# First mixer with every second chunk's keys in reversed token order: one level product for two chunks

## The chip, the cores and the metric

The kernel runs on one core of a Trainium2 chip. The metric is the device time of one execution in microseconds (us). Before the change the median of three runs is 1917.88 us (1913.43 to 1923.1).

TensorE appears as PE (matrix products) and PEld (its weight loads), VectorE as DVE, ScalarE as ACT, SyncE as SP (it issues the weight transfers).

## What is computed

A two-layer decoder trunk (width 1024) takes 512 prompt tokens and 8 sequences of 4 sample tokens. Layer 0 mixes tokens by HGRN2, layer 1 by gated DeltaNet (GDN); a squared-ReLU MLP follows each. The change lies in the HGRN2 mixer, which has 8 heads with 128 key features and 128 value features:

```
S_t = diag(f_t) S_{t-1} + k_t v_t^T        o_t = S_t^T q_t        k_t = (1 - lb) sigmoid(-fz_t)

within a chunk, b = running sum of log f:
A[t, s] = sum_k q[t, k] k[s, k] exp(b[t, k] - b[s, k])     for s <= t
o       = (q exp(b)) S  +  A v
S       = exp(b_last) S +  (k exp(b_last - b))^T v
```

The decay depends on the feature k, so A is no plain product of two matrices.

## The kernel before

Features lie on the 128 partitions, the 544 tokens (T: 512 of the prompt, TP, and 32 of the samples, TS) on the free axis. The prompt is cut into NC = 4 chunks of 128 tokens.

**Levels.** A is built in seven levels, m = 1, 2, 4, ..., 64 (`LEVELS`). At level m each chunk falls into blocks of 2m tokens. The second half of a block (queries) sees its first half (keys), and both decays are taken relative to the last token of the first half, so both exponents stay at or below zero. For a level, VectorE writes the differences (`apart_levels`, lines 1487 and 1488), ScalarE takes their exponential (line 978), VectorE scales queries into `QL` (line 1493) and keys into `KL` (line 1494, `scaled`), PE multiplies (line 509, `level` in `hgrn_rec`), and VectorE copies the wanted pieces into `A` under a mask (`keep`, line 1514, `copy_predicated`). `QL` holds only the second halves, 64 columns a chunk. `KL` keeps the keys at their token's place and zeros at the second halves, so a chunk's product has 128 key rows, half of them zero, and 64 query columns: four products a level, one a chunk. All are in float32, and the hardware runs each such product as two instructions, so a level shows as x8. Levels 1 and 2 have a small product more for the samples (line 512). In the text lv1 ... lv64 are the products of a level on PE, kl1 ... kl64 the pair `QL`, `KL` on VectorE, pred1 ... pred64 the masked copies.

**The diagonal** is a product of keys and queries of each chunk (line 520) times the identity (lines 1524 and 1525).

**One turn of the head loop.** PE runs a head's levels and between them the projections of the next head (`more(n)`: n tiles of six products of 272 columns, line 411; 32 tiles a head). The order on each engine is the order of the program, and semaphores order the engines. The pieces that the text names, by turn:

- the projection of the next head is evacuated in four units: three by line 1440 into `pr` during the turn, the fourth, the values, by line 1440 into `val` at the end of the turn (`hgrn_prepare`, slot 9).
- VectorE writes the low half of each weight tile (`low`, line 1336); PE's tiles of that unit wait for it.
- the forget gate of the next head: ScalarE's chain at lines 927 to 931 (which stands behind the copies at lines 986 and 987, and these behind a small PE transpose, line 449), then VectorE at line 1431 (`fls`), 1452, and the next `low`.
- the end of a turn: the sample state update (line 1553, `snew`), the third evacuation (line 1440), pred64, the scan (1466), `Q` (1468), the next head's level-1 differences, their exponential on ScalarE (961), then the copy of the output (999), its square (1001), PE's sum over features (432, `ss`), ScalarE's reciprocal root (1007, 1011), and VectorE's `out_tail` (1387, 1390, 1392), gate and `val`.
- line 955 on ScalarE writes the next head's keys `K`; lines 1401 and 1402 write `bd`, the distance to the chunk's end.

The first head is prepared ahead of the loop, and the last head stands behind it: there PE's filler is the output projection (14 tiles), and the last levels have none.

## Time and profile before

| quantity | value |
|---|---|
| median of 3 runs | 1917.88 us (1913.43 to 1923.1) |
| profiled execution | 1921.42 us |
| its span, first to last instruction | 1919.6 us, mean granted clock 0.94 |
| PE busy / PEld busy | 1795.0 us (94%) / 1699.2 us (89%) |
| DVE busy | 1089.1 us (57%), 1960 instructions |
| ACT busy | 689.8 us (36%), 1150 instructions |
| diagonal product of the first HGRN2 head to that of the last | 52.76 to 362.45 us |
| the last head's normalised output | 405 us |

The HGRN2 heads take the stretch from about 50 us to about 405 us; the MLPs (PE alone, projections back to back) and the GDN mixer fill the rest. The granted clock is the share of 2.4 GHz that PE was given in a stretch: 1.00 is 2.4 GHz, 0.50 is 1.2 GHz. Whole-span shares say little on a stage of a fifth of the span, so the rows below come from that stage.

### The profile page before, as it was taken

How to read it: one execution, taken by the hardware profiler on the slowest of the kernel's cores; microseconds unless marked ns; L12 is line 12 of the kernel's file. 1: busy time of each engine (PE TensorE's matmuls, PEld its weight loads, DVE VectorE, ACT ScalarE, POOL GpSimd, SP SyncE). 2: the span in 40 equal slices, each digit the busy share in tenths (PEclk: the TensorE clock that was granted, in tenths of full speed). 3: DMA queues.
4: the chain of work that ended last, by engine and by line, in shares of the span. 5: the costliest groups of instructions: out<-in, count | busy, mean ns of one | idle time of the engine just before them, and what ended most of it. 6: DMA issues, size and time to landing. Idle time of an engine off the chain costs nothing. (4 is left out here: it accounts for less than half of the span.)

```text
span 1919.6 us, 33969 instructions
## 1 busy us (share of the span) xinstructions
PE 1795.0 (94%) x13227; PEld 1699.2 (89%) x13227; DVE 1089.1 (57%) x1960; ACT 689.8 (36%) x1150; POOL 0.4 (0%) x5
## 2 busy tenths in 40 slices
PE   6999999989999999987899999999888999999997
PEld 5989999879999898986888888888768999999996
DVE  5777887755444343564567667766724543434344
ACT  5555555422222121223345445544512222222222
POOL 0000000000000000000000000000000000000000
PEclk9989999979999999997899999999758999999997
DMA  5222222213333232331121221122101323333321
GB/s 165 64 70 76 75 78 67 68 58 89 88 88 88 75 88 72 88 79 34 46 58 26 67 58 42 38 58 60 32 24 46 89 88 89 88 88 87 88 76 47
DMA packets 257436, 134.54 MB, mean 70 GB/s; under 512 B 6698, under 2 KB 256004, under 8 KB 257348
## 3 DMA queue, kind: packets, MB, share of 16 engines
q1 hardware_dynamic: 219488, 112.49, 20.6%
q10 hardware_dynamic: 37860, 20.76, 3.8%
q8 instruction: 69, 1.13, 0.2%
q14 instruction: 19, 0.16, 0.0%
HBM read 121.24 MB, written 12.00 MB: 69 GB/s over the span
## 5 line engine op out<-in xcount | busy, mean ns | idle before, releaser
L411 PE MATMUL pj<-xh,w_hi 128*128 128x272 f32 x2064 | 462.2, 306 | 22.2 <-DVE w_lo L1336 9.8
L867 ACT ACTIVATE w_hi<-w_raw 128x1024 fp32r<-128x1024 f32 x209 | 220.7, 1056 | 627.5 <-PE pj L411 624.9
L411 PE MATMUL pj<-xh,w_lo 128*128 128x272 f32 x2064 | 435.7, 293 | 0.0
L411 PE MATMUL pj<-xl,w_hi 128*128 128x272 f32 x2064 | 434.5, 293 | 0.0
L411 PEld LDWEIGHTS pj<-xh,w_hi 128*128 128x128 f32 x2064 | 330.8, 193 | 47.5 <-issue 25.8
L411 PEld LDWEIGHTS pj<-xl,w_hi 128*128 128x128 f32 x2064 | 332.7, 193 | 0.0
L411 PEld LDWEIGHTS pj<-xh,w_lo 128*128 128x128 f32 x2064 | 331.5, 194 | 0.0
L411 PE MATMUL pj<-oh,w_hi 128*128 128x272 f32 x1280 | 269.0, 292 | 14.3 <-DVE ol L1392 7.0
L1336 DVE TENSOR_TENSOR w_lo<-w_raw,w_hi 128x1024 fp32r<-128x1024 f32 x209 | 254.9, 1220 | 44.8 <-ACT w_hi L867 44.8
L411 PE MATMUL pj<-oh,w_lo 128*128 128x272 f32 x1280 | 266.8, 290 | 0.0
L411 PE MATMUL pj<-ol,w_hi 128*128 128x272 f32 x1280 | 265.9, 289 | 0.0
L411 PEld LDWEIGHTS pj<-oh,w_hi 128*128 128x128 f32 x1280 | 203.1, 190 | 18.0 <-DVE ol L1392 7.9
L411 PEld LDWEIGHTS pj<-ol,w_hi 128*128 128x128 f32 x1280 | 203.2, 190 | 0.0
L411 PEld LDWEIGHTS pj<-oh,w_lo 128*128 128x128 f32 x1280 | 201.8, 191 | 0.0
L1832 DVE TENSOR_TENSOR ws<-pj,rstd 128x544 f32<-128x544 f32 x64 | 46.4, 725 | 198.9 <-PE pj L411 194.5
L1844 DVE TENSOR_TENSOR xT<-xT,pj 128x544 f32<-128x544 f32 x48 | 34.6, 721 | 167.9 <-PE pj L411 167.9
L449 PE MATMUL rr<-cf,ws 128*128 128x128 f32 (+2 forms) x440 | 73.2, 305 | 13.3 <-ACT ws L1273 4.8
L449 PEld LDWEIGHTS rr<-cf,ws 128*128 128x128 f32 (+2 forms) x440 | 53.6, 153 | 25.2 <-issue 10.4
L667 PEld LDWEIGHTS rr<-ws 128*128 128x128 f32 x384 | 52.0, 208 | 21.6 <-ACT ws L1192 16.7
L1372 DVE TENSOR_TENSOR xT<-xT,pj 128x544 f32<-128x544 f32 x32 | 23.1, 721 | 81.9 <-PE pj L411 81.9
L667 PE MATMUL rr<-ws 128*128 128x64 f32 x384 | 56.9, 295 | 10.1 <-ACT ws L1192 7.8
L509 PEld LDWEIGHTS rr<-ws 128*128 128x128 f32 x448 | 59.5, 204 | 5.0 <-DVE ws L1494 3.5
(278 smaller groups left out, 2040.8 us busy)
## 6 DMA issues: line engine op xcount, KB each, us to landing
w_raw<-in_mlp_w_up_dram SPq DMA_DIRECT2D x64, 512.0 KB, 3.9
w_raw<-in_mlp_w_down_dram SPq DMA_DIRECT2D x64, 512.0 KB, 3.7
w_raw<-in_hgrn_w_in_dram SPq DMA_DIRECT2D x32, 512.0 KB, 4.0
w_raw<-in_gdn_w_in_dram SPq DMA_DIRECT2D x32, 512.0 KB, 4.2
out_dram<-S ACTq DMA_DIRECT2D x16, 512.0 KB, 3.5
S<-in_state_hgrn_dram ACTq DMA_DIRECT2D x8, 512.0 KB, 4.0
w_raw<-in_hgrn_w_out_dram SPq DMA_DIRECT2D x8, 512.0 KB, 3.6
S<-in_state_gdn_dram ACTq DMA_DIRECT2D x8, 512.0 KB, 4.0
```

The costliest lines, as they stand in the source:

```text
L411: last = mm(pj[:, s, b, 0:HALF], w[:, s, k, :], v[:, k, b * HALF:(b + 1) * HALF], start=(k == 0 and a == 0), stop=(k == KT - 1 and a == 2))
L449: return nc.tensor.transpose(out, in_, cf[0:n, C_EYE:C_EYE + n])
L509: last = mm(rr[:, n % 2, c * 64:(c + 1) * 64], KL[:, n % 2, c * P:(c + 1) * P], QL[:, n % 2, c * 64:(c + 1) * 64], start=True, stop=True)
L667: last = mm(rr[:, 0, c * 64:(c + 1) * 64], NL[:, cols], first_half(Tm[:, cols], m), start=True, stop=True)
L867: f(w_hi[:, c % SPLIT], w_raw[:, slot], ACT.Copy).then_inc(w_high, 1)
L1336: tt(w_lo[:, c % SPLIT], w_raw[:, c % RAW], w_hi[:, c % SPLIT], ALU.subtract).then_inc(w_low, 1)
L1372: tt(halves(xT[:, k]), halves(xT[:, k]), computed(U, r, k), ALU.add).then_inc(unit_out, 1)
L1832: tt(halves(B[:, k % 2]), computed(U, r, k), halves(rstd[:]), ALU.mult).then_inc(unit_out, 1)
L1844: tt(halves(xT[:, k]), halves(xT[:, k]), computed(U, g * (2 * KT), KT + k), ALU.add).then_inc(unit_out, 1)
```

## The change

Chunks 1 and 3 keep their keys, their distances to the chunk's end (`bd`) and their values in reversed token order. Reversing a chunk of 128 turns the first half of every block into the second half of a block. The keys of an even chunk and of the odd chunk behind it therefore fit into one 128-row operand without zeros, and one product of 128 query columns (64 of either chunk) serves two chunks: two products a level in place of four, with the same number of columns.

- `scaled` writes `KL` for the prompt in two pieces, even chunks and odd chunks (reversed decays, second-half places), and in a third for the samples where the level has them. `KL` of the prompt is 256 columns wide where it was 512.
- the evacuation of the values is six instructions where it was one: the four chunks, one of them cut where the PSUM banks meet, and the samples; two of them write backwards.
- `K` on ScalarE is three instructions where it was one; `bd` on VectorE three where it was two.
- `A` is kept by key place, so the diagonal of an odd chunk is an anti-diagonal: it is now a `copy_predicated` under a mask (identity and reversed identity, stored in a mask slot that had no reader) in place of a product with the identity. `A` is cleared once at the start.
- the masks of `keep` are built for the new places; GDN's first masked copy reads its mask from the other slot.

On VectorE, where the loop's last turn ends and the last head begins (the same instructions follow one another between any two turns): `ol` is the end of `out_tail`, the first `ws<-pr,ng` the gate, `ws<-pj,rstd` the values. Before:

```order
L1392 TENSOR_TENSOR ol<-ws,oh 128x544
L1293 REGISTER_ALU
L1480 TENSOR_TENSOR ws<-pr,ng 128x544
L1440 TENSOR_TENSOR ws<-pj,rstd 128x544
L1860 REGISTER_ALU
L1860 COMPARE_AND_BRANCH
```

With the change:

```order
L1403 TENSOR_TENSOR ol<-ws,oh 128x544
L1304 REGISTER_ALU
L1496 TENSOR_TENSOR ws<-pr,ng 128x544
L1499 TENSOR_TENSOR ws<-pj,rstd 128x128
L1500 TENSOR_TENSOR ws<-pj,rstd 128x16
L1501 TENSOR_TENSOR ws<-pj,rstd 128x112
L1502 TENSOR_TENSOR ws<-pj,rstd 128x128
L1503 TENSOR_TENSOR ws<-pj,rstd 128x128
L1504 TENSOR_TENSOR ws<-pj,rstd 128x32
L1893 REGISTER_ALU
L1893 COMPARE_AND_BRANCH
```

One instruction has become six, with the same 544 elements. A little further on, the operands of level 2: first the differences of level 4, then `QL` and `KL` of level 2, then the masked copy of level 1. Before:

```order
L1487 TENSOR_TENSOR ws<-ws 128x64x4
L1488 TENSOR_TENSOR ws<-ws 128x64x4
L1493 TENSOR_TENSOR ws<-ws 128x272
L1494 TENSOR_TENSOR ws<-ws 128x136x2
L1514 COPY_PREDICATED ws<-cu,rr 128x256
L1517 COPY_PREDICATED ws<-cu,rr 32x16
```

With the change:

```order
L1510 TENSOR_TENSOR ws<-ws 128x64x4
L1511 TENSOR_TENSOR ws<-ws 128x64x4
L1516 TENSOR_TENSOR ws<-ws 128x272
L1520 TENSOR_TENSOR ws<-ws 128x64x2
L1521 TENSOR_TENSOR ws<-ws 128x64x2
L1523 TENSOR_TENSOR ws<-ws 128x8x2
L1544 COPY_PREDICATED ws<-cu,rr 128x256
L1547 COPY_PREDICATED ws<-cu,rr 32x16
```

Two instructions more at levels 1 and 2, one more at the other levels. The diff, with what surrounds it left out:

```diff
@@ shape_constants
+        back = (c < TP // 2) & (c // (P // 2) % 2 == 1)
+        row = np.where(back, P - 1 - p[:, None], p[:, None])
+        cu[:, 0, n] = (row // (2 * m) == local) & (row // m % 2 == 0)
+        cu[:, 1, n] = hit & (rh[:, None] == (1 if n else 0))
+    cu[:, 1, -1] = 0
+    cu[:, 1, -1, 0:P] = np.eye(P)
+    cu[:, 1, -1, P:2 * P] = np.eye(P)[::-1]
@@ hgrn_rec, level (PE)
-                    for c in range(NC):
-                        last = mm(rr[:, n % 2, c * 64:(c + 1) * 64], KL[:, n % 2, c * P:(c + 1) * P],
-                                  QL[:, n % 2, c * 64:(c + 1) * 64], start=True, stop=True)
+                    for q in range(NC // 2):
+                        pair = slice(q * P, (q + 1) * P)
+                        last = mm(rr[:, n % 2, pair], KL[:, n % 2, pair], QL[:, n % 2, pair], start=True, stop=True)
@@ hgrn_prepare, slot "K" (ACT)
-                    s.did(f(hg["K"], pr[:, 1, 0:T], ACT.Exp, bias=hc[:, 2:3]), "K")
+                    K, src = hg["K"], pr[:, 1, 0:T]
+                    f(blocks(K[:, 0:TP], P)[:, 0::2, :], blocks(src[:, 0:TP], P)[:, 0::2, :], ACT.Exp, bias=hc[:, 2:3])
+                    f(blocks(K[:, 0:TP], P)[:, 1::2, ::-1], blocks(src[:, 0:TP], P)[:, 1::2, :], ACT.Exp, bias=hc[:, 2:3])
+                    s.did(f(K[:, TP:T], src[:, TP:T], ACT.Exp, bias=hc[:, 2:3]), "K")
@@ hgrn_prepare, slot "scan" (DVE)
-                    v.did(less_than_last(hg["bd"], hg["b"]), "bd")
+                    b, bd = (blocks(hg[name][:, 0:TP], P) for name in ("b", "bd"))
+                    end = b[:, :, P - 1:P].broadcast_to([P, NC, P])
+                    tt(bd[:, 0::2, :], end[:, 0::2, :], b[:, 0::2, :], ALU.subtract)
+                    tt(bd[:, 1::2, ::-1], end[:, 1::2, :], b[:, 1::2, :], ALU.subtract)
...
@@ hgrn_prepare, slot 9 (DVE)
-                    evacuate(3, hg["val"])
+                    ps, val = computed(U_HIN, h * 4, 3), hg["val"]
+                    edge = HALF - 2 * P
+                    tt(val[:, 0:P], ps[:, 0, 0:P], rstd[:, 0:P], ALU.mult)
+                    tt(val[:, 2 * P:HALF], ps[:, 0, 2 * P:HALF], rstd[:, 2 * P:HALF], ALU.mult)
+                    tt(val[:, HALF:3 * P], ps[:, 1, 0:P - edge], rstd[:, HALF:3 * P], ALU.mult)
+                    tt(val[:, P:2 * P][:, ::-1], ps[:, 0, P:2 * P], rstd[:, P:2 * P], ALU.mult)
+                    tt(val[:, 3 * P:TP][:, ::-1], ps[:, 1, P - edge:TP - HALF], rstd[:, 3 * P:TP], ALU.mult)
+                    tt(val[:, TP:T], ps[:, 1, TP - HALF:HALF], rstd[:, TP:T], ALU.mult).then_inc(unit_out, 1)
@@ scaled (DVE)
-                return tt(first_half(KL[:, n % 2, 0:w], m), first_half(K[:, 0:w], m), first_half(dd[:, n % 2, 0:w], m),
-                          ALU.mult)
+                out = KL[:, n % 2, 0:TP // 2].rearrange("p (q n two m) -> p q n two m", q=2, two=2, m=m)
+                keys, fall = (x[:, 0:TP].rearrange("p (q h n two m) -> p q h n two m", q=2, h=2, two=2, m=m)
+                              for x in (K, dd[:, n % 2]))
+                tt(out[:, :, :, 0], keys[:, :, 0, :, 0], fall[:, :, 0, :, 0], ALU.mult)
+                last = tt(out[:, :, :, 1], keys[:, :, 1, :, 1], fall[:, :, 1, ::-1, 0, ::-1], ALU.mult)
+                if m in SLEVELS:
+                    last = tt(first_half(KL[:, n % 2, TP:T], m), first_half(K[:, TP:T], m),
+                              first_half(dd[:, n % 2, TP:T], m), ALU.mult)
+                return last
@@ hgrn_head (DVE)
-                tt(blocks(A[:, 0:TP], P), blocks(rr[:, 2, :], P), over_chunks(eye), ALU.mult)
-                v.did(tt(A[0:TS, TP:T], rr[0:TS, 3, 0:TS], cf[0:TS, C_EYE:C_EYE + TS], ALU.mult), "adiag")
+                diagonal = mask[:, 1, len(LEVELS) - 1, 0:2 * P]
+                pred(over_pairs(A[:, 0:TP]), diagonal.unsqueeze(1).broadcast_to([P, 2, 2 * P]), over_pairs(rr[:, 2, :]))
+                v.did(pred(A[0:TS, TP:T], diagonal[0:TS, 0:TS], rr[0:TS, 3, 0:TS]), "adiag")
```

## Rows read from the trace of the kernel before

**Rows 1.** Stretches, diagonal product to diagonal product: length; busy, instructions by engine; clock, DMA.

```profile
core 0: us, PE busy (x) PEld busy (x) DVE busy (x) ACT busy (x) POOL busy (x), PEclk, DMA share, GB/s
96.01:143.33 47.32, 46.53 (x322) 42.48 (x321) 35.35 (x71) 23.70 (x39) 0.00 (x0) 0.89 0.24 68
...
187.43:231.56 44.13, 43.34 (x323) 40.63 (x322) 35.25 (x71) 23.73 (x39) 0.00 (x0) 0.96 0.26 73
231.56:274.16 42.60, 41.81 (x323) 39.11 (x322) 35.25 (x71) 23.73 (x39) 0.00 (x0) 1.00 0.26 75
```

**Rows 2.** Waits of PE's weight loads, 96 to 364 us: total, times, longest.

```profile
PEld pj L411 <- DVE w_lo L1336: 5.2, 12, 0.5
...
PEld rr L509 <- DVE ws L1494: 3.5, 6, 0.6
```

**Rows 3.** Timeline of PE in an undisturbed turn: start, length, instruction, idle before.

```profile
237.33 1.00 PE L509 MATMUL rr<-ws 128*128 128x64 f32 x8
238.26 0.23 PE L512 MATMUL rr<-ws 128*32 128x16 f32 x2
241.69 1.10 PE L509 MATMUL rr<-ws 128*128 128x64 f32 x8 [0.36 <-DVE ws L1494]
...
252.39 0.52 PE L411 MATMUL pj<-xh,w_hi 128*128 128x272 f32 x2 [0.30 <-DVE w_lo L1336]
...
264.62 1.00 PE L509 MATMUL rr<-ws 128*128 128x64 f32 x8
...
274.16 1.05 PE L520 MATMUL rr<-ws 128*128 128x128 f32 x8
275.14 0.25 PE L521 MATMUL rr<-ws 128*32 128x32 f32 x2
```

**Rows 4.** Timeline of DVE in the same turn.

```profile
235.75 0.72 DVE L1440 TENSOR_TENSOR ws<-pj,rstd 128x544 f32<-128x544 f32 x1
...
241.21 0.42 DVE L1494 TENSOR_TENSOR ws<-ws 128x272 f32<-128x272 f32 x1
241.56 0.71 DVE L1514 COPY_PREDICATED ws<-cu,rr 128x256 f32<-128x256 uint8 x1
...
249.72 0.73 DVE L1431 SCALAR_TENSOR_TENSOR ng<-pr,ng 128x544 f32<-128x544 f32 x1 [2.11 <-ACT ng L931]
...
263.40 1.20 DVE L1553 TENSOR_TENSOR S<-S,rr 128x1024 f32<-128x1024 f32 x1
264.82 0.72 DVE L1440 TENSOR_TENSOR pr<-pj,rstd 128x544 f32<-128x544 f32 x1 [0.23 <-PE pj L411]
265.71 0.45 DVE L1514 COPY_PREDICATED ws<-cu,rr 128x256 f32<-128x256 uint8 x1 [0.17 <-PE rr L509]
...
274.48 0.79 DVE L1387 SCALAR_TENSOR_TENSOR ws<-ws,vec 128x544 f32<-128x544 f32 x1 [2.64 <-ACT ws L1011]
```

**Rows 5.** Timeline of ACT in the same turn.

```profile
247.33 0.27 ACT L986 ACTIVATE vTs<-rr 32x128 f32<-32x128 f32 x1 [2.14 <-PE rr L449]
...
263.25 0.76 ACT L955 ACTIVATE ws<-pr,hc 128x544 f32<-128x544 f32 x1 [1.85 <-DVE ws L1494]
...
269.53 0.60 ACT L999 ACTIVATE ws<-rr 128x512 f32<-128x512 f32 x1 [0.18 <-PE rr L564]
```

**Rows 6.** Timeline of DVE in the GDN mixer, an evacuation from PSUM in pieces.

```profile
1134.06 0.40 DVE L1596 TENSOR_TENSOR xp<-pj,rstd 128x240 f32<-128x240 f32 x1
1134.38 0.18 DVE L1597 TENSOR_TENSOR xp<-pj,rstd 128x32 f32<-128x32 f32 x1
1134.47 0.43 DVE L1595 TENSOR_TENSOR xp<-pj,rstd 128x272 f32<-128x272 f32 x1
```

**Rows 7.** Timeline of PE in the last head, levels 32 and 64.

```profile
385.99 1.95 PE L509 MATMUL rr<-ws 128*128 128x64 f32 x8
...
391.57 1.97 PE L509 MATMUL rr<-ws 128*128 128x64 f32 x8
```

**Rows 8.** A stretch of two microseconds in the turn of 187.43, columns as in rows 1.

```profile
220.00:222.00 2.00, 2.00 (x10) 2.00 (x10) 0.47 (x1) 0.00 (x0) 0.00 (x0) 0.50 0.85 239
```

**Rows 9.** Forty microseconds of the GDN mixer, columns as in rows 1.

```profile
1130.00:1170.00 40.00, 37.16 (x270) 33.87 (x269) 28.46 (x67) 18.88 (x45) 0.00 (x0) 0.96 0.24 68
```

More of the change, by code:

```diff
@@ L87, in shape_constants @@
         hit = rb[:, None] == local[None, :]
-        cu[:, 0, n] = hit & (rh[:, None] == 0)
-        cu[:, 1, n] = hit & (rh[:, None] == 1)
+        back = (c < TP // 2) & (c // (P // 2) % 2 == 1)
[5 more added lines that the diff above has]
+    cu[:, 1, -1, P:2 * P] = np.eye(P)[::-1]
     return cf, cu.reshape(P, -1)
@@ L305, in blocks, with over_pairs @@
             return ap.rearrange("p (n m) -> p n m", m=m)
+        def over_pairs(ap):
+            return ap.rearrange("p (q r) -> p q r", r=2 * P)
         def width(m):
@@ L1296, in _ @@
             nc.vector.memset(epsc[:], EPS).then_inc(unit_out, 2)
-            for buf in (hg["KL"], hg["QL"], gt4[:], gcol[:], dtb[:], xp[:]):
+            for buf in (hg["KL"], hg["QL"], hg["A"], gt4[:], gcol[:], dtb[:], xp[:]):
                 nc.vector.memset(buf, 0.0)
@@ L1470, in hgrn_prepare @@
                     v.did(apart_levels(0, 1), "d1")
-                    v.did(less_than_last(hg["bd"], hg["b"]), "bd")
+                    b, bd = (blocks(hg[name][:, 0:TP], P) for name in ("b", "bd"))
+                    end = b[:, :, P - 1:P].broadcast_to([P, NC, P])
+                    tt(bd[:, 0::2, :], end[:, 0::2, :], b[:, 0::2, :], ALU.subtract)
+                    tt(bd[:, 1::2, ::-1], end[:, 1::2, :], b[:, 1::2, :], ALU.subtract)
+                    b = hg["b"][:, TP:T]
+                    v.did(tt(blocks(hg["bd"][:, TP:T], SLEN), last_of(b, SLEN), blocks(b, SLEN), ALU.subtract), "bd")
                 if slot == 7:
@@ L1522, in hgrn_head @@
                 differences(1, 2)
-                after(t, "diag", h)
-                tt(blocks(A[:, 0:TP], P), blocks(rr[:, 2, :], P), over_chunks(eye), ALU.mult)
-                v.did(tt(A[0:TS, TP:T], rr[0:TS, 3, 0:TS], cf[0:TS, C_EYE:C_EYE + TS], ALU.mult), "adiag")
+                ready = fixed(dve, t.after("diag", h))
+                dve.wait_ge(c_in, 16 * N_CONST)
+                dve.wait_ge(t.sem, ready)
+                diagonal = mask[:, 1, len(LEVELS) - 1, 0:2 * P]
+                pred(over_pairs(A[:, 0:TP]), diagonal.unsqueeze(1).broadcast_to([P, 2, 2 * P]), over_pairs(rr[:, 2, :]))
+                v.did(pred(A[0:TS, TP:T], diagonal[0:TS, 0:TS], rr[0:TS, 3, 0:TS]), "adiag")
                 after(sa, "ebd", h)
@@ L1693, in gdn_prepare @@
                     dve.wait_ge(v.sem, ready)
-                    pred(second_half(Tt[:, 0:TP], 1), blocks(mask[:, 0, 0, 0:TP // 2], 1), second_half(NL[:, 0:TP], 1))
-                    v.did(pred(second_half(Tt[0:TS, TP:T], 1), blocks(mask[0:TS, 0, 0, TP // 2:T // 2], 1),
+                    pred(second_half(Tt[:, 0:TP], 1), blocks(mask[:, 1, 0, 0:TP // 2], 1), second_half(NL[:, 0:TP], 1))
+                    v.did(pred(second_half(Tt[0:TS, TP:T], 1), blocks(mask[0:TS, 1, 0, TP // 2:T // 2], 1),
                                second_half(NL[0:TS, TP:T], 1)), "tt1")
```

## The prediction

> **What bounds the kernel now.** The change touches only the HGRN2 heads, so I leave the whole-span chain of waits aside and cut that stage at its diagonal products. The stretches by engine [rows 1] are turns of the head loop: look at PE's busy time against the length. PE is busy 41.81 of 42.60 us in the turn without a disturbance, VectorE 35.25 of the same. So PE looks like the bound, with little room. Second view, PE's waits [rows 2]: over six turns its weight loads wait 5.2 us for low halves of weights (twelve times, so twice a turn) and 3.5 us for the operands of a level (six times). PE therefore does not run free: at three places of each turn VectorE comes last already. Third view, the timelines of one undisturbed turn on PE, DVE and ACT [rows 3 to 5]: they show which places these are, and whether a faster PE could pull the other engines along.
>
> Walk the turn from the level-2 product (lv2). It starts at 241.69 after a wait for kl2, and kl2 started at 241.21, in a run of VectorE without a gap from the output's normalisation through the values [rows 3, 4]. Then the forget gate: ScalarE waits 2.14 us for PE's small transpose, VectorE 2.11 us for ScalarE, then writes the low half for which PE waits 0.30 us at 252.39 [rows 3 to 5]. From 249.72 on VectorE runs without a gap to the sample state at 263.40, and the next three idle pieces are short: 0.23 us for PE's tiles, 0.17 us for lv64, and 0.18 us on ScalarE for the output [rows 4, 5]. So a chain of PE, ScalarE and VectorE sets the turn, and PE's 98% is mostly its filler.
>
> **Prices.** On PE, eight instructions of 64 columns take 0.93 us (237.33 to 238.26), eight of 128 columns 0.98 us (274.16 to 275.14) [rows 3]. Columns cost next to nothing here, instructions do: a level of four takes 0.49 us, and each level saves 0.44 us. Over 7 levels and 8 heads PE is relieved of 24.6 us.
>
> On VectorE the elements stay the same and instructions are added. The pieces of a PSUM evacuation give the price: 240 columns take 0.32 us from start to start, 32 take 0.09 [rows 6], so a column costs 1.1 ns and an instruction by itself about 0.06 us. The values (one to six) cost 0.32 us more a turn, kl2 (two more) 0.13 us, kl16, kl32 and kl64 (one more each) 0.19 us together. The page "VectorE: DVE Perf Modes" of the Trainium skill (section on the TRN2 errata) gives a PSUM source 120 cycles of fixed cost, 0.125 us; by that the values would cost 0.63 us and seven turns 2.1 us more. The 32-column row, 0.09 us in all, leaves no room for that, and I stay with the row.
>
> No row shows an operand read or written backwards, or such short pieces of two strided halves. The nearest is the masked copy, which takes 0.71 us for 256 elements in runs of one and 0.45 us in runs of 64 [rows 4]: a bad pattern can cost 0.13 us on 128 elements, while kl2 with runs of two takes 0.42 us, as the plain ones do. I take nothing, and keep 0.13 us a piece as the upper end; the other end is nothing too, since no element is saved. The diagonal turns from a product into a masked copy of 512 elements in long runs: equal, upper end 0.5 us a turn.
>
> **The sum, for a turn.** (a) *From the end of one head to lv2.* VectorE leads, so its 0.45 us (values and kl2) make the turn longer. What lv1 saves on PE becomes a longer wait. (b) *lv2 to the forget gate.* ScalarE waits for PE, so lv2 and lv4 count in full: -0.88 us. (c) *Forget gate to the low half.* ScalarE and VectorE lead; lv8's 0.44 us goes into the wait of 0.30 us. (d) *VectorE without a gap to the sample state:* +0.19 us. lv16, lv32 and lv64 are relieved where PE is not last. (e) *End of the turn.* PE now arrives early, so the three idle pieces go: -0.58 us; late next is ScalarE's chain behind the third evacuation. Together 0.45 - 0.88 + 0.19 - 0.58 = **-0.82 us** a turn, **-5.7 us** in seven.
>
> *Covers.* bd and kl1 (0.19 us more) lie before VectorE's idle 2.64 us, kl4 and kl8 before its 2.11 us [rows 4]. The three pieces of K on ScalarE cost at most 0.5 us and have 1.85 us of idle time before them [rows 5], on a chain that goes on with the third evacuation. If these covers went, the pieces would cost 0.3 us and 0.5 us a turn. Clearing A once at the start costs under a microsecond before the first projections; the masks have the same size, so the transfer is the same, and GDN's copy reads another slot at the same price.
>
> *The slow stretches.* In six of the seven turns a part runs at half clock, 1.2 GHz [rows 1, 8], in the usual turn behind the state products between lv32 and lv64; it makes the turn 44.13 instead of 42.60 us, 1.53 us. At that place PE was last by 0.23 us and will be early: 0.88 (lv16, lv32) + 0.19 - 0.23 = 0.84 us. So much of each stretch is now hidden: 6 x 0.84 = **-5.0 us**.
>
> *The last head.* No next head, less filler, and half clock in lv32 and lv64, which took 1.95 and 1.97 us [rows 7]: these save up to 0.9 us each, the five others 0.44 us each. The ends are 2.2 us (the slow two gain nothing, since their operands come last) and 4.0 us; I take **-3.3 us**, nearer the upper, because PE is the engine with the queue there.
>
> Sum: -5.7 - 5.0 - 3.3 = -14.0 us on the profiled execution's 1921.4 us. That one lies 3.5 us above the median, as much as two slow stretches; with two fewer the relief is 1.7 us smaller. So 1917.9 - 12.3 = **1905.5 us**.
>
> **Rivals.** *VectorE's pieces are dearer, or the stretches are not hidden.* VectorE has six reversed or strided pieces on the path of a turn (two values, four kl); at 0.13 us each they eat the whole 0.82 us, and 1905.5 + 5.5 = 1911 us is left. The diagonal at its upper end, or three of the slow stretches moving to where PE is last, do about as much. For it: no row shows the pattern. Against: kl2's price with runs of two.
>
> *PE's whole relief counts.* If VectorE has slack that the gapless runs hide, up to 24.6 us come: 1893 us. Against it: the waits of rows 2, which exist before PE is relieved.
>
> *The clock falls at the new waits.* PE will idle about 1.8 us before lv2, where it now waits 0.4 to 0.6, about 0.7 us at the low half, and 0.7 us before the features' sum. If the clock falls once a turn before lv2, a stretch of 1.53 us lands on the path of (b): 7 x 1.53 = 10.7 us, and 1916 us is left. For it: slow stretches start behind thin work. Against: the GDN mixer, where PE is idle 2.8 us of 40 and gets 0.96 [rows 9], the same as here. The page "TensorE: Matmul & The Clock Gate" of the Trainium skill (section on HAM oscillation) says the same as this rival: waits between short bursts bring the half clock back each time round. So far the trace bears it out only at thin products, not at waits of this size.
>
> *Slower: the clock falls for a long part of every turn.* PE's work in a turn will be 41.81 - 7 x 0.44 = 38.7 us at full clock, and about 3.2 us of waits. At the clock of the turn of 96 us, 0.89 [rows 1], that is 38.7 / 0.89 + 3.2 = 46.7 us against today's 44.1, 2.6 us a turn: 18 us in seven, less the last head's 3.3: about 1933 us. It decides from a granted clock of about 0.91 as the mean of the turns. One turn of seven does this today, and the gap before lv2 would have to make it the rule.
>
> *The change does nothing on PE.* Two products of 128 columns for four of 64 would bring nothing if columns set the time; the two prices of rows 3 speak against it, and I give it no chance of its own.
>
> **How the numbers follow.** Runs of this kernel differ by 0.5% from lowest to highest, and 0.5% (9.6 us: below 1908.3 faster, above 1927.5 slower) is about what can be told from no change. Chances: the forecast 0.52 (1899 to 1910, so 0.47 faster and 0.05 the same); dearer pieces or unhidden stretches 0.20 (0.05 faster, 0.15 the same); the whole relief 0.08 (faster); the clock falling once a turn 0.12 (0.11 the same, 0.01 slower); the clock falling for long 0.08 (slower). That is 0.60 faster, 0.31 the same, 0.09 slower. The range of 1894 to 1917 us takes in the forecast, the dearer pieces, most of the single falls and half of the whole relief, and leaves out about 0.17.
>
> **What the profile of the changed kernel would show.** Levels as x4 of 128 columns from 0.5 us each. The values as six pieces in about 0.95 us. PE's wait before lv2 grown from about 0.5 to some 1.8 us, and the waits for the low half grown; PE's busy share of a turn down by about 3 us while the turn shrinks by 1 to 2 us. VectorE without the 0.23 and 0.17 us of idle time at the end of a turn. Turns with a slow stretch 42.5 us and less, those without one about 41.8. The forecast is wrong if the wait before lv2 does not grow (then more of PE's relief counts), if a piece of kl or of the values takes over 0.3 us, or if half clock shows before lv2.

## The result, and the profile after

| | before | after |
|---|---|---|
| median (runs) | 1915.66 us (4; 1912.29 to 1923.1) | 1884.24 us (4; 1878.22 to 1890.1) |
| ratio, 95% interval | | 0.9824 [0.9806, 0.9842] |
| span of the profiled execution | 1919.6 us | 1878.4 us |
| seven turns, first to last diagonal product | 309.69 us | 291.54 us |
| last diagonal product to GDN's first product of decays (last head, output projection, first MLP) | 572.8 us | 556.2 us |
| GDN mixer / the rest behind it | 502.3 / 482.1 us | 495.8 / 482.3 us |

The change makes the kernel 31.4 us faster; 12.3 were forecast, and 1884 lies outside the range of 1894 to 1917. The spans of the two profiled executions differ by 41.2 us: the turns give 18.15, the stretch behind them 16.6, GDN 6.5. The last of these goes with the execution more than with the change: over all profiles of this study GDN took between 495.7 and 504.2 us, and both 504.2 and 495.8 for one and the same kernel (kd_later, below). A second profile of either kernel (below) gave turns of 306.47 and 291.66 us and 572.7 and 556.2 us behind them: 14.8 and 16.5 us, together 31.3, about the difference of the medians.

The page's first part, after; beside the table in front PE lost 47 us of busy time (about 22 from fewer products, by the 2.76 us that a turn shows below and eight heads; most of the rest is full clock in place of half), VectorE gained 7 us and 121 instructions:

```profile
PE 1748.0 (93%) x13003; PEld 1652.6 (88%) x13003; DVE 1096.1 (58%) x2081; ACT 692.2 (37%) x1166; POOL 0.4 (0%) x5
```

**The turns.** The windows of an undisturbed turn and of a turn with a stretch at half clock, to hold against [rows 1]:

```profile
core 0: us, PE busy (x) PEld busy (x) DVE busy (x) ACT busy (x) POOL busy (x), PEclk, DMA share, GB/s
134.07:175.70 41.63, 39.05 (x294) 36.01 (x293) 36.07 (x86) 23.98 (x41) 0.00 (x0) 1.00 0.27 77
175.70:218.28 42.58, 40.49 (x295) 37.45 (x293) 36.15 (x86) 24.06 (x41) 0.00 (x0) 0.96 0.27 76
```

PE is busy 2.76 us less than in the undisturbed turn of before, yet the turn is only 0.97 us shorter (42.60 to 41.63): the rest is now waiting. PE's waits over six turns, to hold against [rows 2], show for what. The low halves cost 12.3 us where they cost 5.2; the operands of a level 4.3 where they cost 3.5; the sum over features (L440) is new.

```profile
PEld pj L419 <- DVE w_lo L1347: 12.3, 12, 1.1
...
PEld rr L518 <- DVE ws L1523: 4.3, 6, 0.7
...
PEld rr L440 <- ACT ws L1012: 2.7, 4, 0.7
```

PE's timeline in the undisturbed turn from 134.07, the places of [rows 3]:

```profile
134.07 1.05 PE L528 MATMUL rr<-ws 128*128 128x128 f32 x8
139.84 0.61 PE L518 MATMUL rr<-ws 128*128 128x128 f32 x4
...
143.16 0.52 PE L419 MATMUL pj<-xh,w_hi 128*128 128x272 f32 x2 [0.85 <-DVE w_lo L1347]
144.67 0.71 PE L518 MATMUL rr<-ws 128*128 128x128 f32 x4 [0.50 <-DVE ws L1523]
...
154.59 0.52 PE L419 MATMUL pj<-xh,w_hi 128*128 128x272 f32 x2 [0.77 <-DVE w_lo L1347]
...
172.42 1.18 PE L440 MATMUL rr<-ws,ones 128*128 128x272 f32 x4 [0.46 <-ACT ws L1012]
175.70 0.49 PE L528 MATMUL rr<-ws 128*128 128x128 f32 x3
```

And VectorE's in the same turn, the places of [rows 4]: the values in six pieces (L1502 writes backwards), the diagonal as a masked copy, the pieces of kl2, the forget gate, and at the end the third evacuation and pred64 without the idle time ahead of them.

```profile
138.26 0.28 DVE L1499 TENSOR_TENSOR ws<-pj,rstd 128x128 f32<-128x128 f32 x1
138.46 0.17 DVE L1500 TENSOR_TENSOR ws<-pj,rstd 128x16 f32<-128x16 f32 x1
...
138.72 0.28 DVE L1502 TENSOR_TENSOR ws<-pj,rstd 128x128 f32<-128x128 f32 x1
...
139.22 0.44 DVE L1510 TENSOR_TENSOR ws<-ws 128x272 f32<-128x272 f32 x1
...
139.92 0.73 DVE L1557 COPY_PREDICATED ws<-cu,rr 128x512 f32<-128x512 uint8 x1
...
144.06 0.27 DVE L1520 TENSOR_TENSOR ws<-ws 128x128 f32<-128x128 f32 x1
144.26 0.27 DVE L1521 TENSOR_TENSOR ws<-ws 128x128 f32<-128x128 f32 x1
144.46 0.15 DVE L1523 TENSOR_TENSOR ws<-ws 128x16 f32<-128x16 f32 x1
...
151.92 0.73 DVE L1442 SCALAR_TENSOR_TENSOR ng<-pr,ng 128x544 f32<-128x544 f32 x1 [2.11 <-ACT ng L939]
...
165.79 1.20 DVE L1586 TENSOR_TENSOR S<-S,rr 128x1024 f32<-128x1024 f32 x1
166.92 0.70 DVE L1451 TENSOR_TENSOR pr<-pj,rstd 128x544 f32<-128x544 f32 x1
167.55 0.43 DVE L1544 COPY_PREDICATED ws<-cu,rr 128x256 f32<-128x256 uint8 x1
```

**The first MLP.** The change touches nothing there, and about 15 us went there. What PE waits for in 610 to 810 us, before the change; in the same window after it no wait of PE's loads is listed at all:

```profile
PEld pj L411 <- DVE w_lo L1336: 5.4, 2, 2.7
PEld pj L411 <- issue: 4.3, 2, 2.2
```

The timeline of PE's loads before the change, at the end of a pass of the MLP's loop (`group(g)` in a loop on PE), shows these as two halts, one behind the other, at the back-branch:

```profile
640.43 0.32 PEld L411 LDWEIGHTS pj<-oh,w_lo 128*128 128x128 f32 x2
643.45 0.30 PEld L411 LDWEIGHTS pj<-xh,w_hi 128*128 128x128 f32 x2 [2.70 <-DVE w_lo L1336]
...
646.47 0.50 PEld L411 LDWEIGHTS pj<-xh,w_hi 128*128 128x128 f32 x2 [2.23 <-issue]
```

What holds PE in the first of them is the branch itself. The view of the loop's line on PE's sequencer gives the shortest, the median and the longest of its three branches in ns, before the change and then after it. Before, the two that go back take 4.54 and 4.56 us, and the one that leaves the loop 0.08 us; after the change the two take 0.21 and 0.22 us.

```profile
L798 PEldq COMPARE_BRANCH  x3: 79/4535/4560, 638.7 to 845.6; - x3
```

```profile
L806 PEldq COMPARE_BRANCH  x3: 76/208/221, 617.6 to 810.0; - x3
```

The windows around the halts, columns as above: 20 us with the halt, and the 7 us behind it, which run at half clock (0.52).

```profile
640.00:660.00 20.00, 15.48 (x102) 15.07 (x101) 4.53 (x5) 2.78 (x3) 0.00 (x0) 0.83 0.20 57
...
645.00:652.00 7.00, 5.53 (x24) 5.53 (x25) 0.00 (x0) 0.00 (x0) 0.00 (x0) 0.52 0.25 70
```

The same 20 us after the change, 162 products in place of 102:

```profile
640.00:660.00 20.00, 20.00 (x162) 20.00 (x161) 10.89 (x14) 5.31 (x7) 0.00 (x0) 1.00 0.27 79
```

The DMA view shows what came meanwhile: between 610 and 810 us before the change the instruction queue q8 moved 17 packets; after it that queue has no line in this window. VectorE's low half is named as the releaser of the first halt because it ended last; PE's loads go on some 0.25 us behind the end of the branch in both passes.

```profile
q8 instruction: 17, 0.28, 0.6%
```

So before the change PE fetches its code again at every back-branch of this loop, and after it does not. The runs below test that.

### The profile page after: what moved, and what is told of

Read it like the earlier page. It is cut to its first block and busy times, and to the rows that moved or that the text cites. A ratio compares the mean times of both kernels' runs of the same rounds, so it can differ in the third digit from the quotient of the medians.

```text
span 1878.4 us, 33666 instructions
## 1 busy us (share of the span) xinstructions
PE 1748.0 (93%) x13003; PEld 1652.6 (88%) x13003; DVE 1096.1 (58%) x2081; ACT 692.2 (37%) x1166; POOL 0.4 (0%) x5
## 5 line engine op out<-in xcount | busy, mean ns | idle before, releaser
L419 PE MATMUL pj<-xh,w_hi 128*128 128x272 f32 x2064 | 457.0, 303 | 21.2 <-DVE w_lo L1347 13.1
L419 PE MATMUL pj<-xh,w_lo 128*128 128x272 f32 x2064 | 430.7, 290 | 0.0
L419 PE MATMUL pj<-xl,w_hi 128*128 128x272 f32 x2064 | 429.7, 290 | 0.0
L419 PEld LDWEIGHTS pj<-xh,w_hi 128*128 128x128 f32 x2064 | 326.6, 191 | 44.7 <-issue 20.9
L419 PEld LDWEIGHTS pj<-xl,w_hi 128*128 128x128 f32 x2064 | 328.0, 191 | 0.0
L419 PEld LDWEIGHTS pj<-xh,w_lo 128*128 128x128 f32 x2064 | 326.5, 191 | 0.0
L457 PEld LDWEIGHTS rr<-cf,ws 128*128 128x128 f32 (+2 forms) x440 | 53.6, 152 | 25.3 <-issue 10.2
L675 PEld LDWEIGHTS rr<-ws 128*128 128x128 f32 x384 | 52.0, 208 | 21.6 <-ACT ws L1203 16.7
L1639 DVE SCALAR_TENSOR_TENSOR pr<-xp,hcw,pr 128x568 f32<-128x568 f32 x72 | 58.2, 809 | 3.9 <-ACT pr L1061 2.2
```

The costliest lines, as they stand in the source:

```text
L419: last = mm(pj[:, s, b, 0:HALF], w[:, s, k, :], v[:, k, b * HALF:(b + 1) * HALF], start=(k == 0 and a == 0), stop=(k == KT - 1 and a == 2))
L457: return nc.tensor.transpose(out, in_, cf[0:n, C_EYE:C_EYE + n])
L675: last = mm(rr[:, 0, c * 64:(c + 1) * 64], NL[:, cols], first_half(Tm[:, cols], m), start=True, stop=True)
L1639: v.did(stt(out=pr[:, row, 0:YW], in0=xp[:, row, j:j + YW], scalar=hcw[:, j, g:g + 1], in1=pr[:, row, 0:YW], op0=ALU.mult, op1=ALU.add), f ...
```

## The experiments

All times beside one another in a line come from profiled executions; medians are of the timed runs. "Undisturbed" is a turn at clock 1.00, "hits" counts stretches at half clock in the seven turns (a turn can have two), "behind" is from the last diagonal product to GDN.

| kernel | undisturbed turn | seven turns | hits | behind | median or single time |
|---|---|---|---|---|---|
| before | 42.60 | 309.69 | 6 places, one of them three times as long | 572.8 | 1915.66 |
| before, again | 42.59 | 306.47 | 6 | 572.7 | 1918.17 |
| before_pad144 | 42.60 | 306.49 | 6 | 556.3 | 1903.14 |
| before_pad32 | 42.60 | 306.54 | 6 | 558.7 | 1907.58 |
| two128 | 40.96 | 287.76 | 2 | 554.7 | 1875.88 |
| four64_pad144 | 43.07 | 310.99 | 7 | 556.2 | 1909.27 |
| after | 41.63 | 291.54 | 2 | 556.2 | 1884.24 |
| after, again | 41.65 | 291.66 | 2 | 556.2 | 1883.62 |
| after_pad112 | 41.64 | 292.52 | 3 | 570.3 | 1898.99 |
| after_pad64 | 41.64 | 292.57 | 3 | 555.4 | 1880.54 |
| four_at_16_32 | 41.83 | 297.26 | 4 | 555.3 | 1886.8 |
| four_elsewhere | 42.41 | 301.17 | 4 | 557.4 | 1902.25 |
| kd_later | 40.36 | 285.79 | 4 | 555.2 | 1875.15 |
| kd_later, again | 40.36 | 285.82 | 4 | 555.0 | 1873.3 |

**1. Where TensorE's code stands.** The change takes 112 instructions out of PE's program ahead of the first MLP (two written-out heads, seven levels, two products, four instructions each). Theory: the 15 us hang on the place of the MLP's code alone. The same number of tiny products at PE's start puts it back:

```diff
@@ PE's program, at its start (28 in after_pad112, 36 in before_pad144)
             pe.wait_ge(ones_set, 1)
+            for _ in range(28):
+                mm(rr[0:1, 3, 0:1], ones[:, 0:1], ones[:, 0:1], start=True, stop=True)
             first_unit(U_HIN, "n0")
```

> The changed kernel, with 28 tiny float32 products (112 instructions) put in front of PE's program, as many instructions as the change took out of PE's code ahead of the first MLP; PE waits for the first transfer there anyway. Placement theory: some 15 us of the gain come from the first MLP, whose PE loop was fetched again in each pass before the change and lies in place after it, because its code has moved; with the old place the fetches and the halts at the loop's end come back: the first MLP 15 us longer, 1899 us, HGRN turns still 41.6 us. Rival, the MLP gains because the mixer leaves it in a better state (weights loaded ahead, clock): 1884 us, no halts.

> The kernel before, with 36 tiny float32 products (144 instructions) in front of PE's program, which puts the code behind the HGRN heads at the same place in a block of 256 instructions as the change does (112 fewer). Placement theory: the halts in the first MLP go, 1916 - 15 = 1901 us, HGRN turns still 42.6 to 44.1 us. Rival, the mixer's state: 1916 us, the halts stay.

Measured: the change with 112 instructions more takes 1898.99 us, 14.75 more than the change (ratio to before 0.9897 [0.9872, 0.9922]); the kernel before with 144 more takes 1903.14 us (0.9926 [0.9899, 0.9954]). One has the packets, the halts and two branches of 4.66 and 4.50 us; in the other they are gone, and the branches take 0.21 us. The waits of PE's loads in the first MLP of after_pad112, 610 to 810 us:

```profile
PEld pj L419 <- DVE w_lo L1350: 5.6, 2, 2.8
PEld pj L419 <- issue: 4.6, 2, 2.8
```

So 15 us of the result are a matter of place. With like placement the change itself is worth 19.5 us (before 1918.52 to 1898.99, timed side by side), or 18.9 (1903.14 to 1884.24, from two sets of runs).

**2. Which places fetch.** A packet is 16 KB (1.13 MB in 69), and one comes in some 16 us, in which PE issues some 256 instructions. Counting the program gave a rule, which two more paddings (8 and 16 tiny products, the same edit) test:

> The kernel before with 8 tiny products (32 instructions) at TensorE's start and nothing else. A packet of the code queue is 16 KB (1.13 MB in 69), and by the pace of the packets in the first MLP (one in some 16 us, at about 16 instructions a us) a packet is 256 instructions. Counted from the program, the first MLP's loop on TensorE is 1,562 instructions, 6.1 packets; in the kernel before it begins in the last instruction of a packet (3,839 instructions ahead of it) and so touches 8 packets, in the changed kernel (3,727 ahead) it touches 7. Theory A (a loop of 7 packets stays, one of 8 is fetched anew each pass): 32 instructions move the loop's start into the next packet, 7 are touched, no packets between 620 and 800 us, no halts, and the stretch from the last HGRN2 head to the gated DeltaNet is 554 to 558 us and not 570 to 573; the time 1900 to 1905 us. Theory B (it goes with the place in some other way, or with the HGRN2 products themselves): the fetches and the 15 us stay.

> The changed kernel with 16 tiny products (64 instructions) at TensorE's start, where 112 had brought the fetches back. The loop's start then stands 207 instructions into its packet and its end 232 into its last one: 7 packets. Theory A: no fetches, 554 to 558 us for the stretch, the time 1880 to 1886 us. Theory B (code moved towards the place of before fetches again): fetches, 570 us, 1895 to 1900 us.

Both came without packets behind the loop's first pass and without halts, at 558.7 and 555.4 us behind the turns. The first lies just above the 554 to 558 us that were expected, and its time, 1907.58, above the 1900 to 1905, with GDN at 503.7 us in it. The page's line of the code queue: before_pad32 first, then after_pad112.

```profile
q8 instruction: 51, 0.84, 0.2%
```

```profile
q8 instruction: 69, 1.13, 0.2%
```

The traces show the length and the place of the loop, and they are not quite those of the count. One pass has 1,578 instructions on PE (768 weight loads, 768 products and 42 others), 16 more than were counted. Behind each fetching back-branch 14 of them run before the second halt, before the change as in after_pad112; so the loop starts 14 instructions ahead of a packet's edge, and not in a packet's last place. With these two figures the rule still holds: the loop touches eight packets there, and seven with 112 instructions fewer, 48 fewer, 32 more or 144 more. Each of the two passes behind a fetching branch moved nine packets (69 less 51, in two passes), by this count the eight of the loop and one behind it.

So a loop of 1,578 instructions that touches 7 packets stays, and one that touches 8 is fetched anew in each pass. By this length it touches 8 from the 41 last places of a packet's 256. It was fetched at the one place tried among these, and not at three others (112 and 144 fall on the same place of a packet). The edge of the 41 was not tried. The page "Runtime: NRT & Kernel Launch" of the Trainium skill (section on instruction fetch mechanics) gives PE's code store as 128 KiB, 2048 instructions, filled in blocks of 256: the size of a packet agrees with the runs. The same section of the Trainium skill holds that crossing a block is mostly hidden; the trace agrees in the straight run of a pass, where a packet comes every 16 us and no wait is listed. It also says that only two lines are kept, beside a division that is for a store of 32 KiB; for PE's 128 KiB the same division gives eight, an estimate from that page's figures. The runs show seven kept, and two fetching back-branches at some 7.5 us each where eight are touched. Why eight do not stay is not shown.

**3. The two halves of the change, each alone.** First the change with four products of 64 columns a level again (VectorE's pieces stay; 144 instructions in front for the place of the code); then the kernel before with two products of 128 columns (PE's relief without the pieces; every second chunk takes the keys of the one before it).

```diff
@@ level, in four64_pad144 (of the change)
-                    for q in range(NC // 2):
-                        pair = slice(q * P, (q + 1) * P)
-                        last = mm(rr[:, n % 2, pair], KL[:, n % 2, pair], QL[:, n % 2, pair], start=True, stop=True)
+                    for c in range(NC):
+                        cols, pair = slice(c * 64, (c + 1) * 64), slice(c // 2 * P, (c // 2 + 1) * P)
+                        last = mm(rr[:, n % 2, cols], KL[:, n % 2, pair], QL[:, n % 2, cols], start=True, stop=True)
@@ level, in two128 (of the kernel before)
-                    for c in range(NC):
-                        last = mm(rr[:, n % 2, c * 64:(c + 1) * 64], KL[:, n % 2, c * P:(c + 1) * P],
-                                  QL[:, n % 2, c * 64:(c + 1) * 64], start=True, stop=True)
+                    for c in range(0, NC, 2):
+                        last = mm(rr[:, n % 2, c * 64:(c + 2) * 64], KL[:, n % 2, c * P:(c + 1) * P],
+                                  QL[:, n % 2, c * 64:(c + 2) * 64], start=True, stop=True)
```

> The changed kernel with each level as four products of 64 columns again (same operands, same result), and 144 instructions of padding, so that the MLP's code lies as in the changed kernel. It keeps all that VectorE and ScalarE pay and takes back PE's relief. Chain theory (level 2 and level 4 count in full, the three idle pieces at the turn's end come back, levels 32 and 64 make the slow stretches): undisturbed turns 41.6 + 0.88 + 0.58 = 43.1 us, slow stretches in most turns again as before the change, so 18 to 22 us behind the changed kernel: 1902 to 1906 us. Rival, PE is the bound and every level counts: turns 41.6 + 3.1 = 44.7 us, about 1909 us. Rival, the number of slow stretches is chance and has nothing to do with the products: two or three slow turns as in the changed kernel, about 1896 us.

> The kernel before with two products of 128 columns a level in place of four of 64; all else stays as before (every second chunk is multiplied by the keys of the chunk ahead of it, so this leaves out half the key operands). PE's code gets as short as in the changed kernel. It is PE's relief without what VectorE pays. Chain theory: undisturbed turns 42.6 - 0.88 - 0.58 = 41.1 us, half a microsecond below the changed kernel's 41.6, few slow stretches, the halts in the first MLP gone: about 1880 us. Rival, VectorE's added pieces cost nothing on the path: 1884 us, turns of 41.6 us. Rival, PE is the bound and every level counts: turns of 39.5 us, about 1868 us.

Measured: 1909.27 us (0.9964 [0.9944, 0.9984]) and 1875.88 us (0.9774 [0.9748, 0.98]). The first lies above the expected 1902 to 1906 (its ten times go from 1901.6 to 1922.21) and at the 1909 of the rival by which every level counts; but that rival wants turns of 44.7 us, and an undisturbed turn takes 43.07. The second is 4 us faster than expected. By undisturbed turns the four kernels form a square: VectorE's pieces cost 0.47 us with four products (42.60 to 43.07) and 0.67 with two (40.96 to 41.63); PE's relief brings 1.64 us without the pieces and 1.44 with them. The sum in the prediction has 0.64 and 1.46.

**4. The stretches at half clock.** The four-product kernels have them in five or six of the seven turns, the two-product ones so far in two or three. Is it the level products next to the thin work around lv16 and lv32, or the whole turn's load?

```diff
@@ level (of the change; in four_elsewhere the levels 1, 2, 4, 8, 64; tiny products in front: 56 and 44)
-                    for q in range(NC // 2):
-                        pair = slice(q * P, (q + 1) * P)
-                        last = mm(rr[:, n % 2, pair], KL[:, n % 2, pair], QL[:, n % 2, pair], start=True, stop=True)
+                    width_ = 64 if m in (16, 32) else P
+                    for c in range(TP // 2 // width_):
+                        cols, pair = slice(c * width_, (c + 1) * width_), slice(c * width_ // P * P, (c * width_ // P + 1) * P)
+                        last = mm(rr[:, n % 2, cols], KL[:, n % 2, pair], QL[:, n % 2, cols], start=True, stop=True)
```

> Only levels 16 and 32 take four products of 64 columns again, the other five keep two of 128; VectorE's work is that of the change. 56 tiny products at TensorE's start bring the code behind it to where it stands, block for block, in the change (so the first MLP should not fetch again). Theory A (the stretches of half clock come from the level products around 16 and 32 being thin work behind the output's normalization): the stretches are back in five to seven of the seven turns, at about 0.8 to 1.0 us each, and an undisturbed turn is that of the change (41.62 us) to 0.3 us more, since these products stand where TensorE is not waited for at once: about 1889 to 1894 us. Theory B (it is the whole turn's load that decides, wherever it falls): stretches in three or four turns only, 1884 to 1889 us.

> The counterpart: levels 1, 2, 4, 8 and 64 take four products of 64 columns, 16 and 32 keep two of 128; 44 tiny products at TensorE's start for the same place of the code. Theory A: the stretches stay as rare as with the change (two or three of seven turns), while an undisturbed turn is 42.5 to 43.0 us, since levels 2 and 4 pay their 0.44 us each on the path: about 1890 to 1894 us, all of it as undisturbed turns. Theory B: stretches in five to seven turns and turns of 42.5 us or more: 1894 to 1902 us. Neither shows a fetch in the first MLP.

Measured: 1886.8 us (0.9841 [0.9824, 0.9857]) and 1902.25 us (0.9922 [0.9905, 0.9938]), the second profiled with a GDN of 504.2 us. Both have four hits: theory A falls twice, and theory B's count holds for the first and misses for the second. What does stand, with one exception, is where a hit falls: some 23 to 33 us behind the diagonal, from the products of four columns on (for the change, 26 us). The exception is one of the seven in four64_pad144, 11.9 us behind the diagonal. PE's timeline after the change, in a turn that is hit (from 175.70):

```profile
198.71 1.95 PE L556 MATMUL rr<-ws,S 128*128 128x4 f32 x16
...
201.10 0.41 PE L419 MATMUL pj<-xh,w_lo 128*128 128x272 f32 x2
...
202.10 0.66 PE L419 MATMUL pj<-xh,w_lo 128*128 128x272 f32 x2
...
203.92 1.06 PE L518 MATMUL rr<-ws 128*128 128x128 f32 x4
```

And in the turn ahead of it (from 134.07), which is not:

```profile
157.08 1.95 PE L556 MATMUL rr<-ws,S 128*128 128x4 f32 x16
...
160.47 0.41 PE L419 MATMUL pj<-xh,w_hi 128*128 128x272 f32 x2
...
161.22 0.61 PE L518 MATMUL rr<-ws 128*128 128x128 f32 x4
```

From the diagonal to 25.9 us behind it the two turns start the same instructions at the same distances; then one falls to half clock and the other does not. So the content of the turn does not decide alone.

**5. Kernel or chance?** Both kernels once more, unchanged:

> The kernel before once more, unchanged, for a second profile. Theory A (which turns get a stretch of half clock goes with the kernel's own timing): stretches in six of the seven turns again, their sum 308.5 to 310.5 us, the first MLP halting as before. Theory B (it is luck of one execution): two to four turns hit, the sum 303 to 307 us.

> The changed kernel once more, unchanged. Theory A: stretches in two or three of the seven turns again, their sum 291 to 293 us. Theory B: any other number, four to seven hit giving 294 to 298 us. The gated DeltaNet's part, whose products are the same in all kernels, should come out at either 496 or 503 us in both runs of this pair, by chance and not by kernel.

Six and two stretches again, though those of before lie in five turns this time and not in six (one turn has two), and one of the changed kernel's two is in another turn. In the counts of stretches theory A holds: they go with the kernel. In the sum it misses for before by 2 us, and 306.47 is what theory B expected, since the long stretch of the first profile (10.2 us in the turn of [rows 1] from 96.01) did not come again. GDN, expected at 496 or 503, took 499.9 and 497.5: it has no two fixed values. What in a kernel sets the count of stretches stays open; a turn made shorter by a move on VectorE alone (next) has four, in the same four turns in both of its profiles.

**6. VectorE ahead of lv2.** If VectorE's gapless run ahead of lv2 sets the turn, then work there that nobody needs yet can be moved behind kl2: the decayed keys and queries, two instructions of 0.70 us each.

```diff
@@ hgrn_rec, VectorE's order (and TensorE now waits for kd ahead of its transposes)
-                after(sa, "ebd", h)
-                v.did(tt(kd, K, hg["bd"], ALU.mult), "kd")
-                v.did(tt(qe, Q, eb, ALU.mult), "qe")
...
+                        if n == 1:
+                            after(sa, "ebd", h)
+                            v.did(tt(kd, K, hg["bd"], ALU.mult), "kd")
+                            v.did(tt(qe, Q, eb, ALU.mult), "qe")
```

> The change with one thing moved: VectorE writes the decayed keys and queries (kd, qe) behind level 2's operands and no longer ahead of level 2's difference, so its stretch ahead of the level 2 product is shorter by these two instructions, about 1.2 us. Theory A (VectorE's chain up to level 2's operands sets the turn, as the sum of the prediction has it): an undisturbed turn goes from 41.62 to 40.3 to 40.9 us, seven turns give 5 to 9 us, the time 1875 to 1880 us. Theory B (TensorE's own work sets the turn once two products serve a level): undisturbed turns stay at 41.4 to 41.7 us and the time within 0.3% of the change's, 1880 to 1888 us. A third outcome, the transpose of kd coming late and holding the state's product: turns over 41.8 us. The code of TensorE grows by a wait or none, so the first MLP should fetch as little as with the change; if it does fetch, 15 us are to be taken off before the turns are compared.

> The version with kd and qe behind level 2's operands once more. Its profiled execution was the slowest of its five times, with 504.2 us in the gated DeltaNet. Undisturbed turns of 40.3 to 40.4 us again; by theory A four turns hit and a sum of 285 to 287 us, by theory B another number; the gated DeltaNet at 496 to 498 us, which brings the span to some 1873 us.

Measured: 1875.15 us, 9.1 less than the change in another set of runs (0.9781 [0.9765, 0.9798] of before), and 1873.3 in the second profiled execution. Of this the seven turns show 5.8 us (291.54 to 285.79). Theory A holds: an undisturbed turn takes 40.36 us, 1.27 less. This version beats both kernels. Its VectorE, second profile, with the two moved instructions behind kl2:

```profile
142.59 0.27 DVE L1522 TENSOR_TENSOR ws<-ws 128x128 f32<-128x128 f32 x1
142.79 0.16 DVE L1524 TENSOR_TENSOR ws<-ws 128x16 f32<-128x16 f32 x1
142.88 0.71 DVE L1571 TENSOR_TENSOR ws<-ws 128x544 f32<-128x544 f32 x1
143.51 0.70 DVE L1572 TENSOR_TENSOR ws<-ws 128x544 f32<-128x544 f32 x1
```

Its lv2 starts at 143.00, 9.31 us behind its diagonal at 133.69; after the change it was 10.60.

## Why the prediction was wrong

The sum has 14.0 us, all of it in the HGRN2 heads. By the first pair of profiles the heads gave 18.15 in the turns and 1.24 in the last head; by the second pair 14.8 and 2.1. That would have been within the range. What put the time outside is about 15 us in a place that the sum does not have.

**The step that failed** is the first one: "The change touches only the HGRN2 heads, so I leave the whole-span chain of waits aside and cut that stage". On the chip the change also moved the code behind it by 112 instructions, and with it the MLP's loop off a place where PE fetches it anew at each back-branch; that gave 15 us. The trace of before shows the halts (twice 2.7 and 2.2 us, then some 7 us at half clock) in a stretch where PE has no other engine to wait for. PE's waits over the whole span, the time of the loop's branch, the packets of q8 by stretches and a count of the loop's instructions would have made this a term.

**The sum for a turn** held term by term. From the timelines in front and above:

| term | forecast | measured | from |
|---|---|---|---|
| (a) diagonal to lv2 | +0.45 | +0.47 | 10.13 to 10.60 |
| (b) lv2 to the forget gate | -0.88 | -0.78 | 8.03 to 7.25 |
| (c), (d) forget gate to the sample state | +0.19 | +0.19 | 13.68 to 13.87 |
| (e) sample state to the next diagonal | -0.58 | -0.85 | 10.76 to 9.91 |
| a turn | -0.82 | -0.97 | 42.60 to 41.63 |

In (e) the evacuation came 0.29 us earlier behind the sample state and pred64 0.55, more than their idle time in the trace (0.40), and ScalarE's chain gave the rest. The first turn gained more, 1.84 us (41.69 in the second profile of before, 39.85 after); kd_later leaves that turn at 39.85, so VectorE's run ahead of lv2 is not what bounds it. Undisturbed, the seven turns gave 1.84 + 6 x 0.97 = 7.7 us, where -5.7 stood.

**The prices** were nearly right: columns are nearly free on PE (two products of 128 take 0.61 us, where four of 64 took 1.00; from start to start a level saves 0.39 us, where 0.44 stood), a piece on VectorE costs what its row said (six values in 0.96 us; 128 columns written backwards take 0.28 us, as those written forwards), and the masked diagonal took 0.73 us for 0.68. The upper ends for reversed access were not needed, and the first rival falls.

**The slow stretches** (-5.0) were mis-sized. The term let all six stay and become cheaper: 1.53 us each, of which 0.84 are hidden. On the chip a hit costs 0.95 to 0.98 us, so 0.55 to 0.58 are hidden, but there are two where there were six. The relief is 9.2 - 2.0 = 7.2 us by the second pair and 12.4 - 1.9 = 10.5 by the first. That the count would fall was not considered, and how it comes about was not found. The usual place was misread too: the sum puts it between lv32 and lv64, but in the trace of before four of the six begin 26 to 27 us behind the diagonal, ahead of lv32 (27.9).

**The last head** (-3.3, between 2.2 and 4.0) gave 1.24 in the first pair. From its lv1 to the sum over features it gave 2.77 us (28.10 to 25.33), within the ends. Ahead of lv1 it lost 1.53 us: PE's projections ran at half clock there, 0.66 us for a pair in place of 0.41, which the sum did not have. That is no mark of the change alone: before_pad32 has it too (9.62 us from its diagonal to lv1, where before takes 8.31), and two128 and four_elsewhere have not (8.31 and 8.29). PE's timeline after the change in the last head, with lv1, lv32 and lv64; lv64 still runs at half clock, and lv32 no longer does (1.95 us in [rows 7]):

```profile
350.77 0.66 PE L419 MATMUL pj<-ol,w_hi 128*128 128x272 f32 x2
...
353.96 0.61 PE L518 MATMUL rr<-ws 128*128 128x128 f32 x4
...
367.53 0.71 PE L518 MATMUL rr<-ws 128*128 128x128 f32 x4 [0.28 <-DVE ws L1521]
...
372.76 1.22 PE L518 MATMUL rr<-ws 128*128 128x128 f32 x4
```

**The rivals with a falling clock** did not come. The waits ahead of lv2 grew, though less at lv2 itself than forecast (0.85 at the low half and 0.50 at lv2, where 1.8 in one piece was expected), and undisturbed turns keep a clock of 1.00 with them. The page "TensorE: Matmul & The Clock Gate" of the Trainium skill (section on HAM oscillation) tells of longer waits than these, so waits of 0.5 to 0.9 us between full bursts neither bear it out nor speak against it. Half clock did follow longer halts: 2.7 and 2.2 us in the MLP, and 2.5 us ahead of the last head's projections (where before the same 2.46 us had been followed by full clock).

## What to carry to other kernels

Before leaving out the stages that an edit does not touch, ask whether it changes the length of the code ahead of a loop: look for halts at loop ends that no engine explains, at the instruction queue's packets in that stretch, and count how many packets the loop touches; here 32 instructions of padding took 14 us (572.7 to 558.7) off that stretch of the kernel before. Then, when one engine is relieved, follow the intervals from one hand-over to the next: the turn gained 0.97 of 2.76 us, and the interval that grew (VectorE ahead of lv2) was where the next 1.27 us of a turn lay. Stretches at half clock are a term of their own: forecast their count apart from their price.

## What was not expected of the hardware

- A loop of 1,578 instructions on TensorE ran without new fetches at the three places in a packet tried where it touches seven packets of 256 instructions, and was fetched at every back-branch at the one where it touches eight. The branch then took 4.5 to 4.8 us in place of 0.2, and each cost some 7.5 us, of which 4.9 are halt of PE's loads and the rest is half clock behind it.
- Turns made of the same instructions with the same gaps get a stretch at half clock or none, with one exception in the same part of the turn; the number in seven turns repeated from execution to execution in the three kernels profiled twice (six and six, two and two, four and four).
- The GDN mixer of one and the same kernel took 495.8 us in one execution and 504.2 in another.
